# Scan stage of a state-space mixer: the sum over four squares moves from TensorE to GpSimd

## The reference

```python
y = ssd_scan(xs, bm, cm, dt, dt_bias, a_log)            # 32 heads of 64, in 4 groups
y = y + d_skip[:, None] * xs
y = y.reshape(bsz, s_len, D_INNER) * jax.nn.silu(z)     # D_INNER = 2048
y = rmsnorm(y.reshape(bsz, s_len, 4, 512), norm_g)      # mean square over each group of 512 channels
return y.reshape(bsz, s_len, D_INNER) @ w_out
```

## Time and profile before

| | us |
|---|---|
| median of three runs | 3026.98 (3020.18 to 3029.7) |
| the profiled execution's own time | 3024.12 |
| its span, first to last instruction | 3022.4 |
| from the exponentials of pair 2 to the end of pair 15's output | 1381 to 1505, some 4% of the span |
| mean clock granted to TensorE | 0.925 of full speed |

### The profile page before, as it was taken

The page is one execution under the profiler, slowest core; times in us unless marked ns, Lnnn a source line. Parts: engine busy times, 40 slices in busy tenths (PEclk is TensorE's granted clock), DMA queues, the critical chain, the costliest instruction groups (busy, mean ns, idle before and its releaser), DMA issues.

```text
span 3022.4 us, 33796 instructions
## 1 busy us (share of the span) xinstructions
PE 2615.9 (87%) x12580; PEld 2085.5 (69%) x12580; DVE 1412.4 (47%) x1951; ACT 1055.3 (35%) x1489; POOL 220.5 (7%) x245
## 2 busy tenths in 40 slices
PE   7978797779998868898897999969697888799998
PEld 5855676568887757685585887857584666588876
DVE  5754378485552454324635333253525444533323
ACT  2235322215552244235623332232314544333311
POOL 1101112010000000001101000010001111100001
PEclk8979988989999979899997999979789999799999
DMA  6720275242222212220021222222210000122222
GB/s 241 269 84 1 90 258 195 84 139 84 97 97 91 90 45 71 69 86 26 1 91 56 97 97 90 91 69 93 66 56 15 21 14 14 56 85 97 95 84 76
DMA packets 178669, 262.86 MB, mean 87 GB/s; under 512 B 8232, under 2 KB 127904, under 8 KB 178592
## 3 DMA queue, kind: packets, MB, share of 16 engines
q1 hardware_dynamic: 156608, 194.00, 19.8%
q0 software_dynamic: 15232, 58.72, 5.5%
q10 hardware_dynamic: 6752, 9.09, 0.9%
HBM read 255.51 MB, written 2.10 MB: 85 GB/s over the span
## 4 chain that ended last, share of the span: by engine, by line
PE 73%; DVE 14%; ACT 7%; issue 4%; POOL 1%; DMA 1%; DVEq 0%; ACTq 0%; SPq 0%; POOLq 0%
PE ps L668 20%; PE ps L669 20%; PE ps L670 20%; PE ps L1138 2%; PE ps L780 1%; ACT decay L1666 1%; PE ps L822 1%; DVE macc L1880 1%; PE ps L1243 1%; ACT pnt_h L1755 1%; DVE pnt_l L1867 1%; DVE nst L2369 1%; PE ps L1058 1%; DVE wlo L1863 1%; ACT whi L1368 1%
## 5 line engine op out<-in xcount | busy, mean ns | idle before, releaser
L1863 DVE TENSOR_TENSOR wlo<-raw,whi 128x2048 fp32r<-128x2048 f32 x180 | 412.2, 2290 | 822.0 <-ACT whi L1368 821.8
L668 PE MATMUL ps<-acth,wlo 128*128 128x512 f32 x1696 | 671.6, 396 | 38.2 <-DVE actl L1867 26.9
L669 PE MATMUL ps<-actl,whi 128*128 128x512 f32 x1696 | 668.3, 394 | 0.0
L670 PE MATMUL ps<-acth,whi 128*128 128x512 f32 x1696 | 667.1, 393 | 0.0
L1368 ACT ACTIVATE whi<-raw 128x2048 fp32r<-128x2048 f32 x180 | 343.7, 1910 | 712.3 <-PE ps L670 712.3
L668 PEld LDWEIGHTS ps<-acth,wlo 128*128 128x128 f32 x1696 | 324.1, 191 | 109.6 <-issue 41.7
L670 PEld LDWEIGHTS ps<-acth,whi 128*128 128x128 f32 x1696 | 323.5, 191 | 68.6
L669 PEld LDWEIGHTS ps<-actl,whi 128*128 128x128 f32 x1696 | 323.8, 191 | 66.9
L668 PE MATMUL ps<-whi,hid_l 128*128 128x512 f32 x528 | 209.2, 396 | 9.2 <-issue 9.2
L669 PE MATMUL ps<-wlo,hid_h 128*128 128x512 f32 x528 | 207.2, 392 | 0.0
L670 PE MATMUL ps<-whi,hid_h 128*128 128x512 f32 x528 | 207.0, 392 | 0.0
(11 more groups left out here) (324 smaller groups left out, 3821.8 us busy)
## 6 DMA issues: line engine op xcount, KB each, us to landing
mraw<-in_mod_w POOLq DMA_DIRECT2D x48, 1024.0 KB, 5.6
raw<-in_ffn_w_in SPq DMA_DIRECT2D x44, 1024.0 KB, 4.9
raw<-in_ffn_up SPq DMA_DIRECT2D x22, 1024.0 KB, 4.9
raw<-in_ssm_w_in SPq DMA_DIRECT2D x20, 1024.0 KB, 5.0
raw<-in_ffn_w_out SPq DMA_DIRECT2D x20, 1024.0 KB, 5.0
raw<-in_sb_win SPq DMA_DIRECT2D x12, 1024.0 KB, 5.0
raw<-in_ffn_down SPq DMA_DIRECT2D x10, 1024.0 KB, 4.9
raw<-in_xa_wkv SPq DMA_DIRECT2D x8, 1024.0 KB, 5.3
```

The source lines that it names most:

```text
L668: nc.tensor.matmul(o, ll, rh, start=start, stop=False, skip_group_check=True)
L669: nc.tensor.matmul(o, lh, rl, start=False, stop=False, skip_group_check=True)
L670: return nc.tensor.matmul(o, lh, rh, start=False, stop=stop, skip_group_check=True)
L1863: nc.vector.tensor_tensor(wlo[:, slot, :], raw[:, slot, :], whi[:, slot, :].bitcast(F32), ALU.subtract) \
```

## The change

The four squares of a group are added on GpSimd, and TensorE takes one product with `share` a group instead of four. GpSimd does three additions of 128x512 for each group into a third slot of `sq`, 12 in all. To make room, `xdt` becomes two tiles, one of which lies where the last piece of the activations was; GpSimd therefore waits for `cb_ready` before it writes it. TensorE's product for group g now stands behind `pair_output(4g + 6)`; the last one, as before, is ahead of unit 1 of the output projection.

```diff
--- before.py
+++ after.py
@@ -278,8 +278,8 @@
     yl = place("yl", [P, DI // P, SEQ], F32R, at=ARENA + 49152)
     o = ARENA + 81920
     conv4 = place("conv4", [P, 4, SEQ], at=o)
-    sq = place("sq", [P, 2, SEQ], at=o)
-    xdt = place("xdt", [P, 2, TB, P], at=o + 4096); o += 8192
+    sq = place("sq", [P, 3, SEQ], at=o); o += 6144
+    xdt0 = place("xdt0", [P, TB, P], at=o); o += 2048
     group_rstd = place("group_rstd", [P, SEQ], at=o); o += 2048
     skip = place("skip", [P, 2, 2, P], at=o); o += 2048
     acs_t = place("acs_t", [P, SEQ], F32R, at=o); o += 2048
@@ -290,6 +290,7 @@
     o = ACTS
     decay = place("decay", [P, 4, CAUSAL], at=o); o += 4 * CAUSAL * 4
     cbm = place("cbm", [P, 2, CAUSAL], at=o); o += 2 * CAUSAL * 4
+    xdt = [xdt0, place("xdt1", [P, TB, P], at=o)]; o += 2048
     assert o <= ACTS + 32768
 
     wdt = place("wdt", [P, KC, SSM_H], at=WIDE + 8192 - 1024)
...
@@ -1240,20 +1242,19 @@
                         x = tok[:, g, kb, HD * (hd % HPG):HD * (hd % HPG) + HD]
                         off, n = D_OFF[kb], SEQ - P * kb
                         if part == 0:
-                            nc.tensor.matmul(ps[half, bank, P * kb:SEQ], xdt[:, pair % 2, kb, half], decay[:, hd % 4, off:off + n],
+                            nc.tensor.matmul(ps[half, bank, P * kb:SEQ], xdt[pair % 2][:, kb, half], decay[:, hd % 4, off:off + n],
                                              start=kb == 0, stop=False, skip_group_check=True)
                         else:
                             last = nc.tensor.matmul(ps[half, bank, P * kb:P * kb + P], x, skip[:, pair % 2, side, :],
                                                     start=False, stop=kb == TB - 1, skip_group_check=True)
             last.then_inc(pair_y, 1)
 
-        def sum_squares(c):
-
-            pe.wait_ge(y_squared, c + 1)
-            if c % 4 == 0 and c:
-                pe.wait_ge(squares_out, c // 4)
-            nc.tensor.matmul(ps[:, 7, :], share[:], sq[:, c % 2, :], start=c % 4 == 0, stop=c % 4 == 3,
-                             skip_group_check=True).then_inc(squares_in, 1)
+        def sum_squares(g):
+
+            pe.wait_ge(squares_added, 3 * g + 3)
+            if g:
+                pe.wait_ge(squares_out, g)
+            nc.tensor.matmul(ps[:, 7, :], share[:], sq[:, 2, :], start=True, stop=True).then_inc(squares_in, 1)
 
         def scan():
 
@@ -1271,15 +1272,14 @@
                     head_rows(2 * ahead)
                     head_rows(2 * ahead + 1)
                 pair_output(pair)
-                if pair >= 2:
-                    sum_squares(pair - 2)
-            sum_squares(HEAD_PAIRS - 2)
+                if pair % 4 == 2 and pair > 4:
+                    sum_squares(pair // 4 - 1)
 
         def ssm_out():
 
             def before_unit(u):
                 if u == 1:
-                    sum_squares(HEAD_PAIRS - 1)
+                    sum_squares(SSM_G - 1)
                 pe.wait_ge(y_lo, 4 * u + 4)
 
             banks_out()
@@ -1671,12 +1671,13 @@
 
                 act.wait_ge(y_gated, c + 1)
                 if c >= 2:
-                    act.wait_ge(squares_in, c - 1)
+                    taken = c - 1 if c % 4 == 2 else c - 2
+                    act.wait_ge(squares_added, taken - taken // 4)
                 nc.scalar.activation(sq[:, c % 2, :], zt[:, c, :], ACT.Square).then_inc(y_squared, 1)
 
             def root(g):
 
-                act.wait_ge(squares_in, 4 * g + 4)
+                act.wait_ge(squares_in, g + 1)
                 if g:
                     act.wait_ge(y_full, 4 * g)
                 nc.scalar.activation(group_rstd[:], ps[:, 7, :], ACT.Ln, bias=eps_c[:]).then_inc(squares_out, 1)
@@ -2531,7 +2532,21 @@
 
             pool.wait_ge(heads_in, 48)
             pool.wait_ge(acs_lo, 1)
+            def sum_squares(c):
+
+                pool.wait_ge(y_squared, c + 1)
+                if c % 4 == 0:
+                    return
+                if c % 4 == 1 and c > 4:
+                    pool.wait_ge(squares_in, c // 4)
+                total = sq[:, 2, :]
+                nc.gpsimd.tensor_tensor(total, sq[:, 0, :] if c % 4 == 1 else total, sq[:, c % 2, :], ALU.add) \
+                    .then_inc(squares_added, 1)
+                pool.wait_ge(squares_added, c - c // 4)
+
             for pair in range(HEAD_PAIRS):
+                if pair == 1:
+                    pool.wait_ge(cb_ready, 1)
                 if pair >= 2:
                     pool.wait_ge(pair_y, pair - 1)
                 heads_of = slice(2 * pair, 2 * pair + 2)
@@ -2539,10 +2554,14 @@
                                         heads[:, 2, heads_of].unsqueeze(2).to_broadcast([P, 2, P]),
                                         ALU.mult).then_inc(skip_ready, 1)
                 c0 = P * (pair % 4)
-                nc.gpsimd.tensor_tensor(xdt[:, pair % 2, :, :].rearrange("p t (h d) -> p t h d", h=2),
+                nc.gpsimd.tensor_tensor(xdt[pair % 2][:].rearrange("p t (h d) -> p t h d", h=2),
                                         tok[:, pair // 4, :, c0:c0 + P].rearrange("p t (h d) -> p t h d", h=2),
                                         dt[:, :, heads_of].unsqueeze(3).to_broadcast([P, TB, 2, HD]),
                                         ALU.mult).then_inc(xdt_ready, 1)
+                if pair >= 3:
+                    sum_squares(pair - 3)
+            for c in range(HEAD_PAIRS - 3, HEAD_PAIRS):
+                sum_squares(c)
 
         nc.gpsimd.memset(x_in[96:P, 2:4, :], 0.0).then_inc(pool_step, 1)
         pool.wait_ge(pool_step, turns(pool_step))
```

More of the change, by code:

```diff
@@ L451, in build @@
     squares_in = sem("squares_in")
+    squares_added = sem("squares_added")
     squares_out = sem("squares_out")
```

## The result

| | before | changed |
|---|---|---|
| median of nine runs | 3023.99 us (3018.21 to 3029.7) | 3033.69 us (3028.67 to 3040.11) |
| the profiled execution, its span | 3024.12, 3022.4 us | 3028.67, 3027.0 us |

The ratio is 1.0033, with a 95% interval of 1.0021 to 1.0045: 10.0 us slower (6.3 to 13.6). The direction and the two causes were forecast. The forecast of 3042.5 us was 8.8 us too high; some 1.5 us of that is its base, which lay between a profiled execution and a median of three, and the rest lies in its terms.

The account below looks back on a forecast made before the run. The scan was taken as bound by a ring of ACT's exponentials, PE's second row set and the pair's output, no engine being full. 3024.1 + 7.2 + 11.2 - 1.4 = 3041.1 us, 3044.0 on the median; given 3042.5, range 3029 to 3056.

Parts of the forecast that it names:

- the two causes: In the scan: ACT's root waiting for the later product, 7.2 us, and TensorE's clock falling in emptied holes, 11.2 us.
- The twelve products cost nothing where they stood: In PE's idle time in the scan, covered by ACT's exponentials: removing the products itself gives 0.
- The root waits for the late product: At steps 7 and 11 ACT's root waits for the later product, delaying the next exponentials: 2 x 3.6 = 7.2 us lost.
- The clock: In PE's emptied holes: falls behind both long holes and five of nine others, 7 x 1.6 = 11.2 us lost.
- The end of the scan: Two products behind the last output go: 1.4 us gained; another 0.9 us ahead of `pair_output(15)` counted as 0.
- a collision of tile 13's addition with `mix`: At step 15 GpSimd's addition beside DVE's second `mix` delays `gate(14)` by 0.85 us, eating the 0.9 us gain.
- GpSimd's additions cost nothing: Twelve additions at 1.04 us may stretch `mix` by 0.85 each, hidden in DVE's wait for the pair's output: zero.
- the rival that only the long holes fall: Clock falls only in the two long holes behind pairs 6 and 10: 3033.1 us; chance 0.12.
- the clock holds: No clock fall in the scan's emptied holes, only the root's wait: 3029.9 us; chance 0.06.
- nothing shows: The root's wait in the scan is absorbed and the change does nothing that shows: 3022.7 us; chance 0.05.
- PE's order is the bound: The scan's ring passes through the product, each removal worth 1.12 us: faster, 3009 us; chance 0.04.
- GpSimd holds DVE: Additions stretch DVE's `mix` beyond its waits in the scan, up to 10.2 us more: 3051 us; chance 0.08.

Follow-up runs that it names:

- The early product: Changed kernel with each group's product one pair earlier, behind the output of pair 4g+5; ratio to before 1.0035 (1.0019 to 1.0051).
- the kernel with the early product and the holes filled from pair 2: Changed kernel, product one pair earlier, plus products of no use behind outputs of pairs 2 to 12 lacking a real one; ratio to before 0.9986.
- late product with fillings: Changed kernel, product still behind pair 4g+6, plus products of no use behind every other pair from 2 to 13; ratio to before 1.0011.
- early product without additions: Changed kernel with product one pair earlier, GpSimd's additions removed, product taking only each group's fourth square; ratio to before 1.0020.

## Why the prediction was right, and where its sizes were off

- **The twelve products cost nothing where they stood.** Right. With the clock held, the stretch is 7.93 us with a product in PE's hole and without.
- **The root waits for the late product: 7.2 us.** Right: 3.64 us of waiting, 11.45 + 11.46 - 2 x 7.92 = 7.1 us. The early product takes away exactly this.
- **The clock: seven falls at 1.6 us, 11.2 us.** The mechanism is right and is shown from both sides, by filling the holes of the kernel with the early product and of the one before. The size was off: five stretches, three ordinary and the two behind a root, with 1.6, 1.4, 1.6, 1.6 and 1.6 us of excess, 7.8 us. I had taken five ordinary holes, a choice within bounds of 0 to 9; the clock fell behind the outputs of pairs 3, 7 and 11 and held, with an empty hole, behind those of pairs 2, 4, 5, 8, 9 and 12. I could bound this count and not derive it, and that it came out near is in part luck: with the product only one pair earlier the same holes lost 14.5 us, inside the bound of 18 us but well above 11.2.
- **The end of the scan: 1.4 us won.** Too small: from pair 15's exponentials to `gate_diag` it took 32.0 us before and 29.5 in the changed kernel, 2.5 us. Of these, 1.4 are the two products behind the last output, as forecast, and 0.9 are the product of tile 12 ahead of `pair_output(15)`, which I had counted and then given away to a collision of tile 13's addition with `mix`. That is the step that was wrong. In the changed kernel the two hardly met: I had overlooked that GpSimd waits for `squares_in` ahead of the first addition of a group, here 3.12 us, and `pair_output(15)` followed `gate(14)` at once. In the kernels with the early product they did meet, about as I had drawn it, and it cost nothing either. This is the kernel with the early product and the holes filled from pair 2:

```profile
1491.25 2.88 DVE L2259 TENSOR_TENSOR decay<-decay,cbm 128x1280 f32<-128x1280 f32 x2
...
1492.75 2.51 POOL L2551 TENSOR_TENSOR sq<-sq 128x512 f32<-128x512 f32 x1 [1.97 <-ACT sq L1684]
...
1494.05 0.68 DVE L2264 TENSOR_TENSOR zt<-ps,zt 128x512 f32<-128x512 f32 x1
```

The addition starts 1.50 us behind `mix` and takes 2.51 us, `mix` keeps its 2.88 and `gate` follows it. The end of the scan takes 29.4 us there, and 29.4 without any addition.
- **GpSimd's additions cost nothing.** Right. In the changed kernel they take 1.26 to 1.72 us each, and in the fuller pairs they stretch DVE's work by 1.0 us (5.68 to 6.68), by `mix`, which goes from 2.88 to 3.96; I had taken 0.85. DVE's wait ahead of `gate` is still 1.25 us there, and with the early product the stage has the same length with and without them.
- The sum was 7.2 + 11.2 - 1.4 = 17.0 us; the stage shows 7.1 + 7.8 - 2.5 = 12.4, which lies within the interval of the 10.0 us that the runs give.
- **The rivals.** By the total alone, the rival that only the long holes fall would have won: its 3033.1 us lies nearer to the 3033.69 measured than my 3042.5. The stretches exclude it: three ordinary holes fell in the changed kernel. In the early product's kernel no hole from pair 2's to pair 15's exponentials is longer than 1.95 us, and it lost 14.5 us to the clock. The Trainium skill, "TensorE: Matmul & The Clock Gate", section "Why this matters for your kernels", warns only of longer gaps between bursts of matmuls; these traces do not agree, and they decide. That the clock holds, that nothing shows, that PE's order is the bound, and that GpSimd holds DVE are all excluded by the stretches above.

What stays open: for two kernels (late product with fillings, early product without additions) the total lies 6 us below what the stage adds, beyond the interval of the ratio. In their profiled executions nothing behind the stage makes up for it: from `gate_diag` to the end it took 1496.5 and 1497.5 us, against 1495.9 and 1496.2 before. Of the other executions of these kernels only the times are on record, not the stage. Nor is it settled which empty holes let the clock fall.

## What to carry to other kernels

Work in the idle time of the engine on which the clock depends isn't free to remove, even when the chain of waits doesn't touch it. Before you price such work at nothing, look at the granted clock in the nearest stretches that lack it already. When a result comes one step later in a loop, look at what stands in order behind the instruction that waits for it: here it was the exponentials, on which the loop itself depends. And when two changes come in one, as here the sum and its place, try the place alone; with the early product and the holes filled, GpSimd's additions go with a kernel that is faster than before.

## What the runs showed of the hardware

- In a loop of 7.9 us a turn, with TensorE idle 0.89 us ahead of the rows because a product of 1.1 us stood in the hole, the granted clock was 1.00 in every turn. With that hole empty, 1.94 us, it fell to 0.50 in some turns and not in others, and a slow turn was 0.9 to 3.2 us longer.
- After one fall the next hole can fall as well: in the kernel with the early product three stretches in a row (11.06, 10.65, 11.82 us) were slowed, where the changed kernel at the same pairs had one of 1.4 and one of 1.6 us. Without the two waits of 3.6 us the pattern was another one, and it cost 6.7 us more, nearly what the waits had.
- From pair 2's exponentials on, the pattern of falls repeated to 0.02 us in every stretch in two executions that came there 10.5 us apart; ahead of that point one of them had lost 2.8 us more.
- A GpSimd addition of 128x512 beside DVE's `mix` took 1.71 us and made `mix` 3.96 instead of 2.88 us where it began ahead of it; where it began 1.50 us behind the start of the last `mix`, it took 2.51 us and `mix` stayed at 2.88. No rule is drawn from these two cases.
